# Leaving out the unread products in the two rests between an output product and its norm

## The chip, the cores and the metric

The kernel runs on one core of a Trainium2 chip. The metric is the device time of one execution in microseconds (us). TensorE (PE), VectorE (DVE), ScalarE (ACT) and GpSimd (POOL) each work through a stream of their own and meet at semaphores; SyncE (SP) issues the loads of the weights.

## The reference

The input is 256 tokens of width 2048, with 16 tokens set before them. Two blocks follow one another. What matters here is the end of the first block's mixer and the whole of its feed-forward part:

```
m = hybrid_mixer(rmsnorm(h, g_pre_mix), ...)      # ends in  y @ w_out
h = h + rmsnorm(m, g_post_mix)
f = conv_gated_ffn(rmsnorm(h, g_pre_ffn), ...)    # ends in  (...) @ w_down
h = h + rmsnorm(f, g_post_ffn)
x = h[:, 16:]
h2 = rmsnorm_2(x, norm_mix_g_2)                   # second block: attention branches, expert lookup
```

with `rmsnorm(x, g) = x * rsqrt(mean(x * x) + eps) * g` over the 2048 features of a token. Everything is float32.

## The kernel before

Features lie on partitions and tokens along the free axis, so a matrix product gives 128 output features by up to 272 tokens. The weights stream through four buffers of 128 x 1024 elements (some of 128 x 896). ACT rounds each of these chunks to a high part (`cut` of ACT, line 2430), DVE computes the low part (`cut` of DVE, line 1582), and PE forms each product in three passes: high by high, high by low, low by high (function `three`, lines 985 to 987). ACT may start chunk i only when PE has finished chunk i - 3 (semaphore `gemm`), PE needs both parts (`lo`). One engine's instructions run in the order in which they are written out; there is no scheduler.

A norm that stands behind a whole output needs all 16 row tiles before the next product can start. There are two such places, which the text calls rest 1 (behind `w_out` of the first block, lines 1188 to 1194) and rest 2 (behind `w_down`, lines 1220 to 1226). In each:

1. ACT reads the last output tile, once squared and once scaled (lines 2596, 2597).
2. PE sums the squares over the features, token by token, with products one column wide (`token_squares`, line 1010).
3. ACT takes the root (`token_root`, line 2454), DVE the reciprocal (line 1623), and DVE writes it on a diagonal (line 1627).
4. PE multiplies ones by the diagonal, which puts each token's factor on all partitions in bank 7 (`spread_factor`, line 1018).
5. DVE scales a row and adds it to the residual (`post_row`, lines 1631, 1633), ACT and DVE split the normed row in high and low (lines 2442, 1590), and PE starts the next product with it (`by_rows`: for each of 16 rows, seven output tiles of three passes; it waits on `xlo`).

`keep_busy(o, n)` (line 989) issues n products of the 128 x 128 tile of ones with itself into a bank that nothing reads. It is called with 12 at the very start of the kernel, and in each rest once between steps 2 and 4 (3 products) and once behind step 4 (5 in rest 1, 8 in rest 2). A float32 product of this kind is two instructions in the profile, so 3, 5 and 8 products are 6, 10 and 16 instructions.

Of the kernel before, what the change touches and what calls it, by code (L numbers as in the profile page):

```python
# [506 lines left out]
def build(nc, A, out):  # L507
# [35 lines left out]
    ps = [top.enter_context(nc.psum_tensor(f"ps{i}", [128, 512], F32)) for i in range(8)]  # L543
# [439 lines left out]
    def _(t):  # L983
# [5 lines left out]
        def keep_busy(o, n):  # L989

            for _ in range(n):
                t.matmul(o, ones[:], ones[:], start=True, stop=True)  # L992
# [14 lines left out]
        def token_squares(T, row):  # L1007

            for b, (c, n) in enumerate(blocks(T)):
                last = t.matmul(ps[7][:, b:b + 1], tmp[:, row, c + n - 128:c + n], ones[:, 0:1], start=row == 0 and b == 0, stop=row == 5 and b == len(blocks(T)) - 1)  # L1010
            if row == 5:
                last.then_inc(ms_mm, 1)

        def spread_factor(T, n):

            for b, (c, w) in enumerate(blocks(T)):
                t.wait_ge(diagonal, n + b + 1)
                last = t.matmul(ps[7][:, c:c + w], ones[:], tmp[:, 4, c:c + w], start=True, stop=True)
            last.then_inc(factor, 1)
# [169 lines left out]
        token_squares(TQ, 0)  # L1189
        t.wait_ge(o_sq, 16)  # L1190
        token_squares(TQ, 5)
        keep_busy(ps[6][:, 0:128], 3)
        spread_factor(TQ, 0)
        keep_busy(ps[6][:, 0:128], 5)


        def og(n):
# [23 lines left out]
        token_squares(S, 0)  # L1221
        t.wait_ge(o_sq, 32)
        token_squares(S, 5)
        keep_busy(ps[6][:, 0:128], 3)
        spread_factor(S, 3)
        keep_busy(ps[6][:, 0:128], 8)


        x3 = halves(2, S)
# [343 lines left out]
    def _(v):  # L1573
# [380 lines left out]
        def cos_2(x):  # L1954

            c, _, dst = rotation(x)
            if isinstance(x, tuple):
                v.wait_ge(up, 8 + x[1] + 1)
                v.tensor_tensor(dst, source2(x), c, ALU.mult).then_inc(own.up(), 1)
                return  # L1960
            if x == 0:
                v.wait_ge(made2, 3)
            name, h = TILES2[x]
            if name == "iq" and h >= 4:
                v.wait_ge(idx_s, h - 3)
            v.wait_ge(src, COPIED.index(x) + 1)
            o = ps[BANK2["in2", x]][:, 0:S]
            if name == "sk":
                v.scalar_tensor_tensor(dst, o, 128 ** -0.5, c, ALU.mult, ALU.mult).then_inc(ev2, 1)
            else:  # L1970
                v.tensor_tensor(dst, o, c, ALU.mult).then_inc(ev2, 1)

        def sin_2(x):

            _, s_, dst = rotation(x)
            r = ROPED.index(x)
            turned = swapped[r % NTURN]
            v.wait_ge(d_turn[r % NTURN], 16 * brought(x))
            v.tensor_tensor(turned, turned, s_, ALU.mult).then_inc(own.up(), 1)
            v.wait_ge(own.sem, own.n)  # L1980
            if not isinstance(x, tuple):
                v.wait_ge(ev2, READ2.index(("in2", x)) + 1)
            v.tensor_tensor(dst, dst, turned, ALU.add).then_inc(roped, 1)
# [436 lines left out]
    def _(s):  # L2420
# [252 lines left out]
        def side_2(name, a):  # L2673
# [24 lines left out]
            elif name == "relu":  # L2698
                s.wait_ge(idx_s, a + 1)
                if a >= 2:  # L2700
                    s.wait_ge(idx_w, 4 * (a - 1))
                for i in range(2):
                    s.activation(relu_at(2 * a + i, 0, 384), ps[7 - i][:, 0:384], ACT.Relu).then_inc(idx_r, 1)
            elif name == "exp":
                bs, _, pw, _, st = unit2(a)
                if a >= 2:
                    s.wait_ge(turn2, a - 1)
                s.wait_ge(rowmax2, 2 * a + 2)
                for n, (o, nk) in enumerate(VIEW2):
                    s.activation(pw[:, o:o + nk], bs[:, o:o + nk], ACT.Exp, bias=st[:, 2 * n:2 * n + 1],  # L2710
                                 accum_out=st[:, 2 * n + 1:2 * n + 2]).then_inc(expd2, 1)
            elif name == "scale":
                _, _, pw, _, st = unit2(a)
                s.wait_ge(inv2, 2 * a + 2)
                for n, (o, nk) in enumerate(VIEW2):
                    last = s.activation(pw[:, o:o + nk], pw[:, o:o + nk], ACT.Copy, scale=st[:, 2 * n + 1:2 * n + 2])
                last.then_inc(normed2, 1)
            elif name == "tcopy":
                _, bt, _, pT, _ = unit2(a)
                s.wait_ge(turn2, a + 1)  # L2720
                if a >= 2:
                    s.wait_ge(mixed2, a - 1)
                s.copy(pT, bt[:, 0:384]).then_inc(pt2_ok, 1)
            elif name == "high":
                s.wait_ge(mixed2, a + 1)
                s.copy((oa if a < 8 else ob)[0][:, a % 8, :], mixed_at(a)).then_inc(o_h, 1)
# [374 lines left out]
```

## Time and profile before

| what | us |
|---|---|
| median of 3 runs | 3157.22 |
| lowest, highest | 3156.95, 3158.32 |
| the profiled execution | 3157.26 |
| its span, first to last instruction | 3155.5 |
| PE busy in the span | 3144.1 |
| DVE busy | 2146.6 |
| ACT busy | 1822.5 |

The busy time of PE is that of overlapping instructions: a product of 256 columns is recorded as 0.28 us long, while the next one starts about 0.12 us after it. So the pace of PE is read from the starts, and a full busy share doesn't mean that nothing is lost. The granted clock in the views is the share of full speed at which TensorE's clock was granted: 1.00 is 2.4 GHz and 0.50 is 1.2 GHz.

### The profile page before, as it was taken

The page shows a single profiled execution, that of the slowest core. Times are in us where ns is not written, and L with a number is a line of the kernel's source. Part 1 is how long each engine was busy: PE and PEld are TensorE (multiplying, and loading weights), DVE is VectorE, ACT ScalarE, POOL GpSimd, SP SyncE. Part 2 cuts the span into 40 slices and gives each one's busy share as a digit, 9 for nine tenths or more (in the row PEclk, how much of TensorE's full clock was granted, in tenths as well). Part 3 has the DMA queues.
Part 4 walks back from the last instruction along what each step waited for, and adds up shares of the span by engine and source line. Part 5 has one row for each costly group of instructions (what it writes and reads, how often), then busy time and mean ns, then how long its engine had stood idle before and what let it go on. Part 6 is the DMA issues. An engine that isn't in the chain of part 4 may idle for free.

```text
span 3155.5 us, 58852 instructions
## 1 busy us (share of the span) xinstructions
PE 3144.1 (100%) x24162; PEld 3005.8 (95%) x24162; DVE 2146.6 (68%) x3502; ACT 1822.5 (58%) x2610; POOL 455.7 (14%) x313
## 2 busy tenths in 40 slices
PE   9999999999999999999999999999999999999999
PEld 9999999999999999999999999999999888888887
DVE  7987486666665477665666799855555666668887
ACT  6556464444444455555455578877777544446555
POOL 0001200000000000000000056777771000000000
PEclk9999999999999999999999999999999999999999
DMA  6444557666666656544565577788776777766655
GB/s 227 155 148 134 184 182 231 229 224 229 226 201 195 193 172 207 171 157 167 186 197 198 200 190 195 197 194 194 195 194 194 243 242 241 242 227 224 211 187 173
DMA packets 229564, 627.78 MB, mean 199 GB/s; under 512 B 59344, under 2 KB 78896, under 8 KB 229168
## 3 DMA queue, kind: packets, MB, share of 16 engines
q1 hardware_dynamic: 192000, 623.15, 60.4%
q0 software_dynamic: 36864, 0.15, 3.4%
q8 instruction: 192, 3.15, 0.4%
q10 hardware_dynamic: 432, 0.72, 0.1%
q14 instruction: 76, 0.62, 0.1%
HBM read 601.27 MB, written 21.10 MB: 197 GB/s over the span
## 4 chain that ended last, share of the span: by engine, by line
PE 98%; DVE 1%; ACT 0%; issue 0%; POOL 0%; DVEq 0%; ACTq 0%; POOLq 0%
PE ps L985 32%; PE ps L986 32%; PE ps L987 32%; PE ps L1061 0%; PE ps L992 0%; DVE wl L1582 0%; PE ps L1327 0%; PE ps L1267 0%; PE ps L1065 0%; PE ps L1026 0%; PE ps L1313 0%; PE ps L1286 0%; PE ps L1295 0%; PE ps L1069 0%; PE ps L1119 0%
## 5 line engine op out<-in xcount | busy, mean ns | idle before, releaser
L2430 ACT CAST wh<-raw 128x1024 fp32r<-128x1024 f32 (+3 forms) x1094 | 1137.4, 1040 | 1026.1 <-PE ps L987 1006.7
L1582 DVE TENSOR_TENSOR wl<-raw,wh 128x1024 fp32r<-128x1024 f32 (+2 forms) x863 | 1036.9, 1202 | 366.5 <-ACT wh L2430 364.0
L985 PE MATMUL ps<-xh,wh 128*128 128x256 f32 x3088 | 853.9, 277 | 0.5 <-issue 0.5
L987 PE MATMUL ps<-xh,wl 128*128 128x256 f32 x3088 | 850.1, 275 | 0.0
L986 PE MATMUL ps<-xl,wh 128*128 128x256 f32 x3088 | 850.0, 275 | 0.0
L985 PE MATMUL ps<-xw,wh 128*128 128x258 f32 (+2 forms) x2096 | 591.3, 282 | 1.1 <-issue 1.1
L987 PE MATMUL ps<-xw,wl 128*128 128x258 f32 (+2 forms) x2096 | 588.0, 281 | 0.0
L985 PEld LDWEIGHTS ps<-xh,wh 128*128 128x128 f32 x3088 | 579.7, 188 | 1.9 <-issue 0.7
L986 PEld LDWEIGHTS ps<-xl,wh 128*128 128x128 f32 x3088 | 579.8, 188 | 0.1
L987 PEld LDWEIGHTS ps<-xh,wl 128*128 128x128 f32 x3088 | 579.6, 188 | 0.0
L2960 POOL DMA_INDIRECT table<-w_loose x256 | 397.7, 1553 | 806.6 <-DVE w_loose L2257 651.3
L1582 DVE TENSOR_TENSOR wl<-raw,ph 128x1024 fp32r<-128x1024 f32 x231 | 281.3, 1220 | 224.3 <-ACT ph L2435 199.6
L986 PE MATMUL ps<-xw,wh 128*128 128x258 f32 (+2 forms) x1441 | 404.5, 281 | 0.0
L985 PEld LDWEIGHTS ps<-xw,wh 128*128 128x128 f32 x2096 | 394.5, 188 | 1.6 <-issue 1.2
L987 PEld LDWEIGHTS ps<-xw,wl 128*128 128x128 f32 x2096 | 394.3, 188 | 0.0
L986 PE MATMUL ps<-wl,coefs 128*128 128x512 f32 x941 | 365.9, 389 | 0.0
L987 PE MATMUL ps<-wh,coefs 128*128 128x512 f32 x941 | 365.9, 389 | 0.0
L985 PE MATMUL ps<-wh,coefs 128*128 128x512 f32 x941 | 365.9, 389 | 0.0
L986 PEld LDWEIGHTS ps<-xw,wh 128*128 128x128 f32 x1441 | 270.8, 188 | 0.1
L2435 ACT CAST ph<-raw 128x1024 fp32r<-128x1024 f32 x231 | 232.6, 1007 | 0.0
L985 PEld LDWEIGHTS ps<-wh,coefs 128*128 128x128 f32 x941 | 176.6, 188 | 36.7
L987 PEld LDWEIGHTS ps<-wh,coefs 128*128 128x128 f32 x941 | 176.6, 188 | 36.6
(409 smaller groups left out, 4647.3 us busy)
## 6 DMA issues: line engine op xcount, KB each, us to landing
raw<-in_peer_u SPq DMA_DIRECT2D x256, 512.0 KB
raw<-in_peer_v SPq DMA_DIRECT2D x236, 512.0 KB
raw<-in_w_in SPq DMA_DIRECT2D x172, 512.0 KB
raw<-in_w_up SPq DMA_DIRECT2D x82, 512.0 KB
raw<-in_w_gate SPq DMA_DIRECT2D x80, 512.0 KB
raw<-in_w_down SPq DMA_DIRECT2D x80, 512.0 KB
raw<-in_w_out SPq DMA_DIRECT2D x64, 512.0 KB
table<-tmp SPq DMA_DIRECT2D x32, 512.0 KB, 6.6
```

The lines of the kernel that those rows point to most:

```text
L985: t.matmul(o, lh, rh, start=start, stop=False)
L986: t.matmul(o, lh, rl, start=False, stop=False)
L987: return t.matmul(o, ll, rh, start=False, stop=stop)
L1582: v.tensor_tensor(part_at(wl, i), raw[:, i % RN, 0:cols(i)], high.bitcast(F32), ALU.subtract).then_inc(lo, 1)
L2430: last = s.copy(part_at(wh, i), raw[:, i % RN, 0:cols(i)])
L2435: last = s.copy(ph[:, 2 + i % 2, :], raw[:, i % RN, 0:cols(i)])
L2960: g.indirect_dma_start(out=table, out_offset=bass.IndirectOffsetOnAxis(ap=eidx[q][:, n:n + 1], axis=0), in_=wts[q][:, n:n + 1], in_offset= ...
```

## The change

The four calls of `keep_busy` in the two rests are left out. The one at the start of the kernel stays. No wait, no buffer and no other instruction is touched.

```diff
         token_squares(TQ, 0)
         t.wait_ge(o_sq, 16)
         token_squares(TQ, 5)
-        keep_busy(ps[6][:, 0:128], 3)
         spread_factor(TQ, 0)
-        keep_busy(ps[6][:, 0:128], 5)
...
         token_squares(S, 0)
         t.wait_ge(o_sq, 32)
         token_squares(S, 5)
-        keep_busy(ps[6][:, 0:128], 3)
         spread_factor(S, 3)
-        keep_busy(ps[6][:, 0:128], 8)
```

## Rows read from the trace of the kernel before

**Rows 1.** The page: busy time of PE, and the last chain by engine.
```profile
PE 3144.1 (100%) x24162; PEld 3005.8 (95%) x24162; DVE 2146.6 (68%) x3502; ACT 1822.5 (58%) x2610; POOL 455.7 (14%) x313
...
PE 98%; DVE 1%; ACT 0%; issue 0%; POOL 0%; DVEq 0%; ACTq 0%; POOLq 0%
```

**Rows 2.** Waits of PE, whole span: in total, times, longest.
```profile
PE ps L985 <- issue: 1.6, 2, 1.1
...
PE ps L1018 <- DVE tmp L1627: 0.4, 2, 0.2
```

**Rows 3.** Timeline of rest 1: start, length, engine, line, tiles, [idle before].
```profile
397.74 1.47 PE L1010 MATMUL ps<-ones,tmp 128*128 128x1 f32 x12
...
399.07 0.91 PE L992 MATMUL ps<-ones 128*128 128x128 f32 x6
...
399.87 0.62 DVE L1627 TENSOR_SCALAR tmp<-ident,col 128x128 f32<-128x128 f32 x3
...
400.21 0.83 PE L1018 MATMUL ps<-tmp,ones 128*128 128x128 f32 x6 [0.22 <-DVE tmp L1627]
...
400.90 1.36 PE L992 MATMUL ps<-ones 128*128 128x128 f32 x10
401.14 0.42 DVE L1631 TENSOR_TENSOR mt<-mt,ps 128x258 f32<-128x258 f32 x1 [0.66 <-PE ps L1018]
...
402.75 0.48 DVE L1590 SCALAR_TENSOR_TENSOR xw<-ht,par,xw 128x258 fp32r<-128x258 f32 x1
...
403.33 0.36 PE L985 MATMUL ps<-xw,wh 128*128 128x258 f32 x1 [1.07 <-issue]
```

**Rows 4.** Timeline of rest 2.
```profile
1135.59 0.91 PE L992 MATMUL ps<-ones 128*128 128x128 f32 x6
...
1136.37 0.48 DVE L1627 TENSOR_SCALAR tmp<-ident,col 128x128 f32<-128x128 f32 x2
...
1136.71 0.71 PE L1018 MATMUL ps<-tmp,ones 128*128 128x128 f32 x4 [0.21 <-DVE tmp L1627]
...
1137.26 1.95 PE L992 MATMUL ps<-ones 128*128 128x128 f32 x16
...
1139.12 0.48 DVE L1590 SCALAR_TENSOR_TENSOR xl<-ht,par,xh 128x256 fp32r<-128x256 f32 x1
...
1139.70 0.36 PE L985 MATMUL ps<-xh,wh 128*128 128x256 f32 x1 [0.49 <-issue]
```

**Rows 5.** Stretches: length, busy PE, PEld, DVE, ACT, POOL, granted clock, DMA.
```profile
402.30:403.30 1.00, 0.00 (x0) 0.00 (x1) 0.97 (x4) 0.71 (x2) 0.00 (x0) 1.00 0.00 0
...
1139.20:1139.70 0.50, 0.01 (x1) 0.03 (x1) 0.50 (x3) 0.46 (x1) 0.00 (x0) 1.00 0.98 401
```

**Rows 6.** Stretches behind the last product of the kernel.
```profile
3148.10:3150.40 2.30, 0.01 (x1) 0.00 (x0) 1.80 (x7) 1.83 (x7) 0.00 (x0) 1.00 0.87 314
...
3150.50:3150.60 0.10, 0.00 (x0) 0.00 (x0) 0.10 (x1) 0.10 (x2) 0.00 (x0) 0.79 0.95 369
...
3150.70:3155.50 4.80, 0.00 (x0) 0.00 (x0) 0.79 (x2) 0.58 (x1) 0.00 (x0) 0.50 0.64 231
```

**Rows 7.** Timeline of PE at the start of the kernel.
```profile
1.02 5.49 PE L992 MATMUL ps<-ones 128*128 128x128 f32 x24 [1.02 <-POOL ones L2915]
...
6.58 0.43 PE L986 MATMUL ps<-xw,wh 128*128 128x272 f32 x1
6.80 0.33 PE L987 MATMUL ps<-xw,wl 128*128 128x272 f32 x1
...
7.09 0.29 PE L986 MATMUL ps<-xw,wh 128*128 128x272 f32 x1
7.21 0.29 PE L987 MATMUL ps<-xw,wl 128*128 128x272 f32 x1
```

**Rows 8.** Waits of DVE, then of PE, from 1139.7 to 1177 us.
```profile
DVE wl L1582 <- ACT wh L2430: 0.5, 1, 0.5
...
PE ps L1026 <- DVE mt L1604: 0.4, 1, 0.4
```

## The prediction

> **What bounds the kernel now.** I read four views. First the page: PE is busy for 3144.1 us of 3155.5 and makes up 98% of the chain that ended last [rows 1]. So whatever PE loses is lost to the kernel, and whatever another engine does faster is hidden unless PE waits for it. Second, PE's waits over the whole span: apart from the start of the kernel there is almost nothing. The two waits of line 985, 1.6 us together, and the two of line 1018, 0.4 us together, are the ones that matter here [rows 2], and they are the two rests. Third, the timeline of each rest, to see who releases whom. Fourth, the stretches with the granted clock, because products that nobody reads can have only two effects: they hold up what is queued behind them on PE, or they keep PE active.
>
> What the reader is to see in rest 1 [rows 3]: the squares run from 397.74; the six unread instructions begin at 399.07 and last 0.91, so they end at 399.98. DVE begins the diagonal at 399.87, and the spreading products start at 400.21. They wait 0.22 us for DVE. DVE's first scaled row starts at 401.14, when the spread is done (400.21 + 0.83 = 401.04). The low part of the first normed row is finished at 402.75 + 0.48 = 403.23, and the first product starts at 403.33. The ten unread instructions are over at 400.90 + 1.36 = 402.26, so PE has stood still for 1.07 us when it resumes. Rest 2 is the same [rows 4]: the unread instructions end at 1135.59 + 0.91 = 1136.50, the spread starts at 1136.71, the second batch ends at 1137.26 + 1.95 = 1139.21, the low part is finished at 1139.12 + 0.48 = 1139.60 and the first product starts at 1139.70.
>
> **Part one: what the removed instructions held up.** There are 6 + 10 + 6 + 16 = 38 of them, with recorded stretches of 0.91 + 1.36 + 0.91 + 1.95 = 5.13 us of PE time. None is on the path. The batch before the spread ended 0.23 us (rest 1) and 0.21 us (rest 2) before the spread started, and the spread was released by DVE [rows 3, 4]. The batch behind it ended 1.07 and 0.49 us before the products, which were waiting for DVE's low part. That part started from the spread's end, which doesn't move. Bank 6, which they wrote, is read by nobody here, and DVE reads the factors in bank 7. So the gain is 0.00 us. From below I allow 0.1 us of gain for each rest, the hand-over that lies between the end of DVE's low part and PE's start (403.23 to 403.33, 1139.60 to 1139.70), as a bound for any small effect on PE's queue. I take 0: the wait ends with DVE whether PE was busy before it or not.
>
> **Part two: what PE does instead.** Without them PE is still from the end of the squares to the first product, except for the spread. In rest 1 that is 399.07 to 403.33 = 4.26 us, of which the spread takes 0.83, and the last unbroken gap is 403.33 - 401.04 = 2.29 us. In rest 2 it is 1135.59 to 1139.70 = 4.11 us with 0.71 of spread, and the last gap is 1139.70 - 1137.42 = 2.28 us. Before, the unread instructions left gaps of 1.07 and 0.49 us, and the clock was at 1.00 even in those gaps, which is the level of 2.4 GHz [rows 5].
>
> The trace has one place where PE stops behind full-rate work and stays still: the end of the kernel. From 3148.10 on there is no product. The granted clock is 1.00 until 3150.40, 0.79 in the tenth from 3150.50 to 3150.60, and 0.50, the level of 1.2 GHz, from there on [rows 6]. A share of 0.79 in that tenth puts the step at 3150.56. So the clock fell 2.46 us after the last product. The gaps of 2.29 and 2.28 us are a little shorter, but each stands behind only six or four spreading instructions and another gap of about 1 us, where the end of the kernel had dense products before it. Taken over the whole rest PE is idle for 4.26 - 0.83 = 3.43 and 4.11 - 0.71 = 3.40 us, more than the 2.46 that were enough. I take it that the clock falls in both rests, with a chance of 7 in 10.
>
> The Trainium skill, "TensorE: Matmul & The Clock Gate", section "Why this matters for your kernels", advises against gaps between bursts of matmuls only when they are longer than the last gaps here; read literally it would leave the clock at its high level and the sum at 3157.3. The rows at the kernel's end disagree with that reading, since there 2.46 us were enough.
>
> **Price of a fall.** At the start of the kernel PE runs from 1.02 us at half pace: 24 unread instructions before the first real one at 6.18 are 5.16 / 24 = 0.215 us apart, and the products of 272 columns at 6.58 and 6.80 are 0.22 apart. Those at 7.09 and 7.21 are 0.12 apart [rows 7]. (The granted-clock record has no step there; the spacing shows it.) So PE worked for about 5.9 us, 1.02 to 6.9, before it had its full pace. At half pace a stretch of length c does the work of c / 2, so c / 2 is lost. From above a fall costs 5.9 / 2 = 2.95 us. From below it costs 0, when the clock is back as the products resume. The start is the nearest row and the only one, but it is a single reading of something whose timing against the products I can't see, so I don't take it as a constant. I take the middle between the whole and the half of it, c = 4.4 us, or 2.2 us for each rest. If the clock falls before the spread, the spread takes up to twice its time on top: 0.83 and 0.71 us more at most. I take 0 for it and keep it for the upper end.
>
> **What hides a part.** In rest 2's ramp PE later waits 0.4 us for DVE's sums (line 1604) [rows 8]; a PE that comes later would wait less, if DVE doesn't come later too. But DVE is held by PE there: it waited 0.5 us for ACT's high part, which itself waits for PE to finish a row. With PE at half pace DVE stalls at the same place, and the rows behind it in its order stall too. So between 0 and 0.4 us are given back; I take 0.2, halfway, and nothing for rest 1.
>
> **Sum.** 0 + 2.2 + 2.2 - 0.2 = +4.2 us. The profiled execution took 3157.26 us, 1.76 outside its span of 3155.5, and stands 0.04 over the median of the runs, so 3157.26 + 4.2 = 3161.46, and against the median 3161.4. I predict 3161.4 us, 0.13% over the kernel before.
>
> **The rivals.** A measurement of this kernel can tell about 0.2% from no change, which is 6.3 us.
>
> Rival A, not slower: the clock stays at its high level in both rests. For it: the longest unbroken gaps, 2.29 and 2.28 us, are under the 2.46 us of the end, and the spread between the gaps is work. Against it: the idle time of a rest adds up to 3.4 us. Time 3157.2 us, 3157.0 to 3157.3 with the 0.2 us of possible gain. It decides if the spread and the gap lengths are enough activity. Chance 0.12.
>
> Rival B: only one of the rests loses the clock, or it falls in one execution and not in the other, because the two gaps are nearly as long as the bound. Time 3157.2 + 2.2 = 3159.4, 3158.5 to 3160.2. Chance 0.13.
>
> Rival C, clearly slower: the fall comes early, before the spread, in both rests, and each then costs the start's whole 2.95 us plus the slowed spread: 2 x 2.95 + 0.83 + 0.71 = 7.4, or 3164.7 us. For it: between the squares, which are one column wide, and the spread PE is idle for over 1 us more than it is now. Against it: the clock at the end held for 2.46 us, and from the last dense product at 397.74 to the spread at 400.21 it is 2.47 us, so it would be just at the edge, twice. It crosses 0.2% from 3163.5 on. Chance 0.10.
>
> Rival D, faster: the unread instructions held the spread or the products up in a way that the timeline hides, such as the queue of weight loads. It is worth at most 5.13 us, all of their time, if both were wrongly read, or 3152.1 us. The starts follow DVE's ends by 0.1 us in both rests, which leaves no room for it. Chance 0.01.
>
> **How the numbers follow.** The likeliest case, both rests losing the clock, has 0.64: the same steps with c from 2.9 us (2 x 1.45 - 0.2 = 2.7) to 5.9 us (2 x 2.95 = 5.9) give 3159.9 to 3163.1. Cases A, B and the forecast together have 0.89, and a range from 3156.9 to 3163.8 holds them and the nearer half of C; what is left out is well under 2 in 10, but the low end can't be raised without losing A and the upper bound is set by the price of two falls. Over 0.2% slower: C, 0.10, and a tail of 0.02 of the forecast, so 0.12. Over 0.2% faster: D, and 0.01 for what I don't see, so 0.02. Within 0.2%: 0.86.
>
> **What would show it.** In the profile of the changed kernel: the spread starts released by DVE's diagonal, at the same distance from the squares as before (part one). PE has a gap of about 2.3 us before the first product of each ramp. The granted clock shows 0.50 there or just after it, for 3 to 6 us, and the products in that stretch start about 0.22 us apart instead of 0.12. From the ramps' ends on everything is as before, shifted by 4 us. If the clock is 1.00 throughout both rests and the span is 3155.5, the forecast is wrong and rival A holds. If the spread itself is twice as long, rival C has begun. If the first product of a ramp comes earlier after the squares than before, part one is wrong. If the gap at line 1026 in rest 2's ramp is gone, the part given back is larger than my 0.2.

## The result: 4.2 us slower, and the profile after

| | before | after |
|---|---|---|
| median of 20 runs, us | 3157.21 | 3161.44 |
| lowest, highest | 3156.47, 3158.49 | 3160.22, 3162.45 |
| the profiled execution | 3157.26 | 3161.32 |
| its span | 3155.5 | 3159.5 |
| granted clock, mean | 0.999 | 0.998 |

The ratio is 1.0013, with a 95% interval of 1.0008 to 1.0019: 0.13% slower, within the 0.2% that the prediction called no change, but clear of 1. No execution of after is as fast as the slowest of before. The mean granted clock is 0.997 or 0.998 in each of the twenty executions of after, and 0.999 or 1.000 in each of the 102 executions of the kernel before that were run beside the experiments. The forecast was 3161.4.

PE's busy time and its waits over the whole span of after, against [rows 1, 2]:

```profile
PE 3143.2 (99%) x24124; PEld 3005.2 (95%) x24124; DVE 2146.5 (68%) x3502; ACT 1822.3 (58%) x2610; POOL 456.5 (14%) x313
```
```profile
PE ps L985 <- issue: 4.6, 2, 2.3
PE ps L1018 <- DVE tmp L1623: 2.0, 2, 1.0
```

There are 38 PE instructions fewer, 24124 for 24162. The waits that they covered now show: 4.6 us ahead of the ramps for 1.6, and 2.0 us ahead of the spreads for 0.4. (The ramp is the run of products that starts behind a rest.) These waits cost nothing, since the same time was there before with unread work in it. The loss is in what follows. The timeline of rest 1 in after, against [rows 3] (lines stand up to four lower than before: 1586 is the low part of a normed row, 1590 before, and 1623 the diagonal, 1627 before):

```profile
397.40 1.47 PE L1010 MATMUL ps<-ones,tmp 128*128 128x1 f32 x12
...
399.87 0.83 PE L1018 MATMUL ps<-tmp,ones 128*128 128x128 f32 x6 [1.00 <-DVE tmp L1623]
...
402.40 0.48 DVE L1586 SCALAR_TENSOR_TENSOR xw<-ht,par,xw 128x258 fp32r<-128x258 f32 x1
...
402.99 0.55 PE L985 MATMUL ps<-xw,wh 128*128 128x258 f32 x1 [2.29 <-issue]
403.33 0.42 PE L986 MATMUL ps<-xw,wh 128*128 128x258 f32 x1
403.55 0.42 PE L987 MATMUL ps<-xw,wl 128*128 128x258 f32 x1
...
407.62 0.33 PE L985 MATMUL ps<-xw,wh 128*128 128x258 f32 x1
407.79 0.28 PE L986 MATMUL ps<-xw,wh 128*128 128x258 f32 x1
407.91 0.28 PE L987 MATMUL ps<-xw,wl 128*128 128x258 f32 x1
```

From the squares to the first product it is 402.99 - 397.40 = 5.59 us, as before (403.33 - 397.74 = 5.59). Then the products start 0.22 us apart where they were 0.12 apart. The stretches of both rests show why (length, busy PE, PEld, DVE, ACT, POOL, granted clock, DMA):

```profile
400.00:400.80 0.80, 0.70 (x6) 0.61 (x6) 0.15 (x2) 0.00 (x0) 0.00 (x0) 1.00 0.00 0
400.80:401.00 0.20, 0.00 (x0) 0.00 (x0) 0.19 (x1) 0.00 (x0) 0.00 (x0) 0.72 0.00 0
401.00:407.00 6.00, 4.01 (x19) 4.05 (x20) 5.14 (x12) 1.53 (x3) 0.00 (x0) 0.50 0.15 37
...
407.60:407.80 0.20, 0.20 (x4) 0.20 (x3) 0.00 (x0) 0.00 (x0) 0.00 (x0) 0.71 0.32 126
407.80:410.00 2.20, 2.20 (x21) 2.20 (x20) 1.11 (x2) 2.08 (x3) 0.00 (x0) 1.00 0.02 7
...
1141.50:1141.70 0.20, 0.20 (x2) 0.20 (x3) 0.17 (x2) 0.00 (x0) 0.00 (x0) 0.70 0.00 0
1141.70:1144.90 3.20, 3.20 (x17) 3.20 (x16) 2.94 (x6) 0.51 (x1) 0.00 (x0) 0.50 0.21 23
1144.90:1145.10 0.20, 0.20 (x3) 0.20 (x3) 0.00 (x0) 0.00 (x0) 0.00 (x0) 0.77 0.35 90
```

The granted clock fell to 0.50, which is 1.2 GHz, in both rests. A stretch that shows 0.72 was at the low level for 2 x 0.28 of its length, so the fall in rest 1 was at 400.89 and the return at 407.72; in rest 2 the fall was at 1141.58, just behind the first product at 1141.40, and the return at 1144.99. Products worked at the low level for 4.7 us in the first case (from 402.99) and 3.4 us in the second.

Where the 4.0 us of span come from is told by the distances between five marks on PE, which are differences of starts in the timelines:

| | before | after |
|---|---|---|
| start to first square of rest 1 | 397.74 | 397.40 |
| rest 1, to the first product | 5.59 | 5.59 |
| from there to the squares of rest 2 | 731.15 | 733.20 |
| rest 2, to the first product | 5.22 | 5.21 |
| from there to the last product | 2008.13 | 2010.42 |

The two rests are unchanged. Each stretch behind a rest is longer, by 2.05 and 2.29 us, and most of that lies in its first microseconds: the 22nd product of ramp 1 starts 4.63 us behind the first for 2.55 (407.62 - 402.99 against 405.88 - 403.33), and the 18th of ramp 2 starts 3.60 behind it for 2.04, so 2.08 and 1.56 us. The last stretch differs by another 0.7 us. Nearly all of it lies in one place, 112 us behind rest 2, where the same 140 products take 16.49 us for 15.87 at a granted clock of 1.00 (the first of them and the one that follows the last, before and then after):

```profile
1252.10 0.28 PE L986 MATMUL ps<-oal,wh 128*128 128x256 f32 x1
...
1267.97 0.28 PE L985 MATMUL ps<-oah,wh 128*128 128x256 f32 x1
```
```profile
1255.36 0.28 PE L986 MATMUL ps<-oal,wh 128*128 128x256 f32 x1
...
1271.85 0.28 PE L985 MATMUL ps<-oah,wh 128*128 128x256 f32 x1
```

That is 0.118 us between starts for 0.113. Each of the thirteen traces of this study has one of these two lengths there: 15.87 in before, e5, e9 and e10, 16.49 in the other nine. All seven traces with a fall have the longer one, but so have e7 and e11, whose rests are at full clock. So it doesn't need a fall; whether a fall makes it likelier isn't shown. Over the eight traces with rest 2 at full clock the last stretch lies between 2008.10 and 2009.08 us.

### The profile page after: what moved, and what is told of

Read it like the earlier page. It is cut to its first block, busy times and chain, and to the rows that moved or that the text cites. A ratio compares the mean times of both kernels' runs of the same rounds, so it can differ in the third digit from the quotient of the medians.

```text
span 3159.5 us, 58776 instructions
## 1 busy us (share of the span) xinstructions
PE 3143.2 (99%) x24124; PEld 3005.2 (95%) x24124; DVE 2146.5 (68%) x3502; ACT 1822.3 (58%) x2610; POOL 456.5 (14%) x313
## 4 chain that ended last, share of the span: by engine, by line
PE 98%; DVE 1%; ACT 0%; issue 0%; POOL 0%; DMA 0%; DVEq 0%; SPq 0%; ACTq 0%; POOLq 0%
PE ps L985 32%; PE ps L986 32%; PE ps L987 32%; PE ps L1061 0%; DVE wl L1578 0%; PE ps L1323 0%; PE ps L1263 0%; PE ps L1065 0%; PE ps L1026 0%; PE ps L1309 0%; PE ps L1282 0%; PE ps L1291 0%; PE ps L1069 0%; PE ps L1119 0%; PE ps L1470 0%
## 5 line engine op out<-in xcount | busy, mean ns | idle before, releaser
L2426 ACT CAST wh<-raw 128x1024 fp32r<-128x1024 f32 (+3 forms) x1094 | 1137.1, 1040 | 1030.0 <-PE ps L987 1027.6
L986 PEld LDWEIGHTS ps<-wl,coefs 128*128 128x128 f32 x941 | 176.7, 188 | 36.6
L985 PEld LDWEIGHTS ps<-wh,coefs 128*128 128x128 f32 x941 | 176.7, 188 | 36.6
```

The lines of the kernel that those rows point to most:

```text
L985: t.matmul(o, lh, rh, start=start, stop=False)
L986: t.matmul(o, lh, rl, start=False, stop=False)
L2426: last = s.copy(part_at(wh, i), raw[:, i % RN, 0:cols(i)])
```

## Experiments

What is open is when the clock falls. Two theories: T, the last unbroken gap ahead of the products decides; U, the idle time of the whole rest decides. All runs have 11 timed executions; before has 33 beside the first four and the next four, 21 beside e9 and e10 and 15 beside e11.

### e1 and e2: one batch of unread products kept, the other gone

```diff
 e1, rest 1 (rest 2 alike)            e2, rest 1 (rest 2 alike)
         keep_busy(..., 3)           -        keep_busy(..., 3)
         spread_factor(TQ, 0)                 spread_factor(TQ, 0)
-        keep_busy(..., 5)                    keep_busy(..., 5)
```

> The three unread products ahead of the spread stay in both rests, the ones behind it go. Theory T (the last unbroken gap decides): the gap of 2.3 us ahead of the first product of each ramp is as in the changed kernel, so the clock falls in both rests and the time is that of the changed kernel, 3160.9 to 3161.7 us. Theory U (the idle time of the whole rest decides): idle time per rest is 4.3 - 0.8 - 0.9 = 2.6 us, nearly the 2.46 us after which the clock fell at the kernel's end, so it falls in some executions only: 3158 to 3160 us. If the clock is 1.00 through both rests, 3157.2 us, both are wrong on this.

> The five and eight unread products behind the spread stay, the three ahead of it go. Theory T (the last unbroken gap decides): that gap is 1.07 and 0.49 us as before the change, the clock holds and the time is 3157.2 us. Theory U (idle time of the whole rest): 1.1 + 1.07 = 2.2 us in rest 1 and 1.1 + 0.49 = 1.6 us in rest 2, under 2.46, so it holds as well, 3157.2 us. Over 3158.5 us would speak against both, and say that the front batch is what holds the clock.

Measured: e1 3161.14 us (3160.04 to 3162.04), ratio 1.0012 [1.0003, 1.0021]; e2 3158.96 us (3156.80 to 3160.81), ratio 1.0004 [0.9995, 1.0013]; before 3157.43. So e1 is nearly the changed kernel again, +3.7 us for +4.2: three products ahead of the spread save little or nothing. That is what T expected. But e2 fails both theories. It has the short last gaps of the kernel before, and its executions lie over 4 us. In its profiled one, of 3158.96 us, the clock fell in both rests, and in rest 1 it fell while the unread products were running (timeline, then stretches):

```profile
400.57 2.09 PE L992 MATMUL ps<-ones 128*128 128x128 f32 x10
402.99 0.55 PE L985 MATMUL ps<-xw,wh 128*128 128x258 f32 x1 [0.34 <-issue]
...
1136.97 0.71 PE L1018 MATMUL ps<-tmp,ones 128*128 128x128 f32 x4 [0.99 <-DVE tmp L1625]
1137.52 2.92 PE L992 MATMUL ps<-ones 128*128 128x128 f32 x16
1140.09 0.56 PE L985 MATMUL ps<-xh,wh 128*128 128x256 f32 x1
```
```profile
400.50:400.90 0.40, 0.40 (x6) 0.40 (x6) 0.09 (x1) 0.00 (x0) 0.00 (x0) 1.00 0.00 0
400.90:401.10 0.20, 0.20 (x4) 0.20 (x3) 0.20 (x1) 0.00 (x0) 0.00 (x0) 0.75 0.00 0
...
1138.40:1141.60 3.20, 3.20 (x17) 3.20 (x17) 3.13 (x8) 1.52 (x3) 0.00 (x0) 0.50 0.33 126
```

The reader is to see that the ten instructions take 2.09 us where they took 1.36 [rows 3], and that the sixteen of rest 2 now outlast the gap: the ramp starts 1140.09 - 1134.74 = 5.35 us behind the squares for 5.22. So the fall answers to what came earlier, and the last gap (0.34 us, and none in rest 2) doesn't decide it. T doesn't hold. U's number is wrong as well, since the idle time of e2 was under 2.46 us. What remains of U is that both batches count.

The falls aren't in every execution of e2. Of its eleven, the three fastest, 3156.80 to 3157.56 us, have a mean granted clock of 1.000, the next two 0.999, and the six from 3158.96 us up 0.998. So the time goes with the clock within one kernel too.

### e3 and e4: one rest bare, the other as before

```diff
 e3: rest 1 without both calls, rest 2 as before
 e4: rest 1 as before, rest 2 without both calls
```

> The unread products go in rest 1 only. If the loss is local to each rest (the clock's price), this run costs rest 1's share, 2.4 us by the cold products of the changed kernel (402.99 to 407.72 at half pace), so 3159.6 us, and rest 2 is as in the kernel before. Rival: the loss comes from something that the two rests share or that runs on (the order of loads, a lag of DVE that is made good only later), and then this run has all of it, 3161.4 us, or none.

> The unread products go in rest 2 only. Local theory: 1.7 us, from the products that run at half pace in the changed kernel (1141.58 to 1145.0), up to 2.1 us as the median over executions, so 3158.9 to 3159.3 us, and this and the run with rest 1 bare add up to the changed kernel's 4.2 us. Rival: they don't add up (0 or 4.2 us here).

Measured: e3 3159.88 us (3158.35 to 3160.34), ratio 1.0007 [0.9998, 1.0016]; e4 3159.72 us (3158.21 to 3160.67), the same ratio and interval; before 3157.43. Each costs about half, +2.45 and +2.29, together 4.7 against the 4.2 of both at once, as near as medians that move by half a microsecond allow. The loss is local to each rest, and in the trace of each the clock leaves 1.00 only there, apart from the kernel's end. In e3's trace the low level lasted from 402.30 to 409.12, so products worked at it for 5.96 us, and the stretch from the first product to the squares of rest 2 is 733.76 us long for 731.15. e4's profiled execution lost it early (stretches and timeline):

```profile
1136.40:1136.60 0.20, 0.13 (x1) 0.14 (x1) 0.20 (x2) 0.20 (x1) 0.00 (x0) 0.66 0.00 0
1136.60:1143.20 6.60, 4.32 (x19) 4.06 (x20) 5.28 (x13) 1.53 (x4) 0.00 (x0) 0.50 0.31 86
```
```profile
1136.47 1.22 PE L1018 MATMUL ps<-tmp,ones 128*128 128x128 f32 x4 [0.99 <-DVE tmp L1625]
...
1139.96 0.55 PE L985 MATMUL ps<-xh,wh 128*128 128x256 f32 x1 [2.28 <-issue]
```

Here the spread takes 1.22 us for 0.71 and the rest is 1139.96 - 1134.24 = 5.72 us long for 5.22, all of it on the path. That is the slowed spread of rival C. e6's trace has a slight case of it: the fall came at 400.46, in the spread of rest 1, which took 0.91 us for 0.83.

### e5: far more unread products than fit

```diff
-        keep_busy(ps[6][:, 0:128], 5)      # rest 1, behind the spread
+        keep_busy(ps[6][:, 0:128], 19)
-        keep_busy(ps[6][:, 0:128], 8)      # rest 2, behind the spread
+        keep_busy(ps[6][:, 0:128], 20)
```

> The kernel before with 19 and 20 unread products behind the spread in place of 5 and 8: 28 and 24 instructions more, at 0.12 and 0.112 us 3.4 and 2.7 us of PE time. PE stood still 1.07 and 0.49 us there, so if unread products cost only what outlasts that gap, the ramps start 2.3 and 2.2 us late: 3157.4 + 4.5 = 3161.9 us at an undisturbed clock. Rival: PE had more room than the gaps show (it waits for DVE later in the ramps, so a late start is made good): 3157.4 to 3159 us. Rival: unread products cost their whole time anyway, 6.1 us, 3163.5 us.

Measured: 3161.25 us (3161.00 to 3162.97), ratio 1.0012 [1.0003, 1.0021]; before 3157.58, so +3.7. The clock stays at 1.00 up to the kernel's end. The ramps start at once behind the unread instructions (rest 1, then rest 2):

```profile
400.93 4.49 PE L992 MATMUL ps<-ones 128*128 128x128 f32 x38
405.17 0.37 PE L985 MATMUL ps<-xw,wh 128*128 128x258 f32 x1
...
1139.01 4.63 PE L992 MATMUL ps<-ones 128*128 128x128 f32 x40
1143.39 0.36 PE L985 MATMUL ps<-xh,wh 128*128 128x256 f32 x1
```

The rests are 7.40 and 7.16 us long for 5.59 and 5.22, +1.81 and +1.94, and nothing is made good later (731.06 and 2008.10 us for the stretches behind them). My 4.5 was too high, mostly since the end of a recorded product isn't the time at which the next may start: a product recorded as 0.275 us long is followed after 0.112, so PE has 0.16 us more room in each rest than its record shows. Another 0.2 us is that I took 0.12 us for an instruction in rest 1, where it is 0.112. The last 0.1 us of each rest stays open. So unread products are free while they fit and cost their time beyond that, which is what part one of the prediction rests on.

### e6: half of the unread products

```diff
-        keep_busy(..., 3)  spread_factor(TQ, 0)  keep_busy(..., 5)
+        keep_busy(..., 1)  spread_factor(TQ, 0)  keep_busy(..., 2)
-        keep_busy(..., 3)  spread_factor(S, 3)   keep_busy(..., 8)
+        keep_busy(..., 1)  spread_factor(S, 3)   keep_busy(..., 4)
```

> The kernel before with 1 and 2 products in rest 1 and 1 and 4 in rest 2, in place of 3 and 5, 3 and 8. If the clock's fall is a matter of degree, of how much of a rest PE works, this falls in most executions but not all, and costs between the run with only the products behind the spread (3159.0) and the changed kernel (3161.4): 3159.5 to 3161 us. Rival: few products suffice, if they only break the gaps up: 3157.4 to 3158 us.

Measured: 3159.57 us (3159.34 to 3162.15), ratio 1.0008 [0.9999, 1.0017]; before 3157.58. Eight of eleven executions lie between 3159.34 and 3159.91 and three from 3161.28 up. In the profiled one the clock fell in rest 1 and held in rest 2:

```profile
402.00:407.00 5.00, 3.96 (x18) 4.00 (x19) 4.22 (x10) 1.31 (x3) 0.00 (x0) 0.50 0.16 25
...
1136.00:1139.00 3.00, 2.21 (x18) 1.93 (x17) 1.62 (x4) 1.84 (x4) 0.00 (x0) 1.00 0.33 128
1139.00:1142.00 3.00, 1.62 (x14) 1.46 (x13) 2.84 (x8) 1.06 (x3) 0.00 (x0) 1.00 0.56 166
```

So half the filling gives back about half of the loss, and in the trace it does so because one rest lost the clock and the other kept it. No execution is as fast as the slowest of the kernel before, 3158.97 us, and the three slow ones have a mean granted clock of 0.997 for 0.998 or 0.999. That fits a fall in rest 1 each time and in rest 2 sometimes, but only the profiled execution shows where the falls are.

### e7, e8 and e11: the high parts first

Of the 21 passes of a ramp's first row only seven need DVE's low part of that row. Seven others need the high parts alone, and seven the low part of the weights. The edit puts them in that order, so that PE can start before DVE has finished:

```diff
+                early = norm > 0 and k == 0
+                if early:
+                    t.wait_ge(xhi, 16 * norm + 1)
+                    t.wait_ge(hi, i0 + 1)
+                    for n in range(ROWS):      # high by high
+                        t.matmul(outs[n], row_at(wh, i0, n), rhs[n % 2](0)[0], start=True, stop=False)
+                    taken(i0)
+                    for n in range(ROWS):      # low part of the weights
+                        t.matmul(outs[n], row_at(wl, i0, n), rhs[n % 2](0)[0], start=False, stop=False)
                 t.wait_ge(xlo, 16 * norm + k + 1)
+                if early:                      # low part of the row
+                    for n in range(ROWS):
+                        last = t.matmul(outs[n], row_at(wh, i0, n), rhs[n % 2](0)[1], start=False, stop=False)
...
```

e7 and e11 are this in the kernel before, e8 is this in the changed kernel.

> The kernel before with all its unread products, and in the two ramps the first row's 21 passes in another order: the seven high by high ones first, which need only ACT's high part of the row, then the seven with the weights' low part, then the seven that need DVE's low part. ACT's high part is done at 402.07 + 0.51 = 402.58 and 1138.45 + 0.51 = 1138.96, DVE's low part at 403.23 and 1139.60. So PE can start 0.65 us earlier in rest 1 and, as the unread products end at 1139.21, 0.4 us earlier in rest 2. If nothing behind holds PE, the kernel is 1.0 us faster, 3156.4 us. Rival: PE gets ahead but then waits for DVE's second row or low part of the weights, and nothing is gained: 3157.4 us.

> The same new order of the first row's passes in the changed kernel, without unread products in the rests. The last gap shrinks from 2.3 to 1.6 us in both rests. If the clock's fall hangs on that last gap, it now holds often and the time is under 3158.5 us. If it hangs on the activity of the rest as a whole, the clock falls as before and the time is the changed kernel's less the 1.0 to 1.3 us of the earlier start: 3160.2 us.

> The kernel of the run with the high parts first once more, in a new set of runs. If its gain of 1.2 us was real and is that of the two earlier starts (0.85 and 0.4 us or less), it is again 0.7 to 1.3 us under the kernel before. If it was the luck of one set of executions, 0 to 0.4 us.

Measured: e7 3156.37 us (3155.36 to 3157.12), before 3157.58, ratio 0.9995 [0.9986, 1.0004]; e11 3155.96 us (3155.52 to 3156.77), before 3157.16, ratio 0.9996 [0.9987, 1.0005]; e8 3160.31 us (3158.95 to 3161.18), before 3157.58, ratio 1.0008 [0.9999, 1.0017]. e7's timeline (line 1040 is the first seven passes):

```profile
397.54 1.47 PE L1010 MATMUL ps<-ones,tmp 128*128 128x1 f32 x12
...
400.69 1.36 PE L992 MATMUL ps<-ones 128*128 128x128 f32 x10
402.47 1.07 PE L1040 MATMUL ps<-xw,wh 128*128 128x258 f32 x7 [0.42 <-issue]
...
1133.61 1.24 PE L1010 MATMUL ps<-ones,tmp 128*128 128x1 f32 x8
...
1138.18 1.06 PE L1040 MATMUL ps<-xh,wh 128*128 128x256 f32 x7
```

The rests are 4.93 and 4.57 us long, 0.66 and 0.65 shorter than in the kernel before, 1.31 together. Both sets gave 1.2 us under their runs of before, and in e11 only one of eleven executions isn't under the lowest of before. This is the fastest version of the study by its medians, but each interval includes 1, so a change of 0.04% isn't settled by either interval alone. e8 lies 1.1 us under the changed kernel. Not all of that need be the earlier start, since the low level lasted 3.4 us in both rests of e8's trace, where it was 6.8 and 3.4 us in that of after. Last gaps of 1.64 us for 2.29 didn't hold the clock.

### e9 and e10: the gaps filled to the brim

```diff
 e9 (e7's order):    3 -> 4 ahead of the spreads, 5 -> 7 and 8 behind
 e10 (before's):     3 -> 4 ahead of the spreads, 5 -> 9 and 8 -> 10 behind
```

> The order of the first row's passes of the run with the high parts first, and the rests filled as far as they go without touching the path: four unread products ahead of the spread in place of three, seven behind it in rest 1 in place of five, eight in rest 2 as before. If some executions of the kernel before still lose the clock for a moment in a rest (its times spread over 2 us, those of the overfilled run over half a us but for one), filling holds it, and the median comes down to the low end of the run with the high parts first, 3155.5 to 3155.9 us, with a narrower spread. Rival: the spread comes from elsewhere (the start), and the time is that run's, 3156.4 us. Rival: the fourth product touches the spread and costs up to 0.2 us in each rest.

> The kernel before with four unread products ahead of the spread and nine and ten behind it, in place of three, five and eight, which fills the gaps without outlasting them by more than 0.1 us. If a fuller rest is safer, 3156.8 to 3157.0 us with a narrow spread; if the rests of the kernel before already hold the clock always, 3157.4 us as before.

Measured: e9 3156.76 us (3155.82 to 3157.53), ratio 0.9999 [0.9990, 1.0008]; e10 3157.93 us (3156.66 to 3158.43), ratio 1.0002 [0.9993, 1.0011]; before 3157.01. Neither is better than the kernel that it fills, and neither spread is narrower, so the guess that the kernel before still loses the clock at times has nothing for it. In e9's trace the rests are 4.94 and 4.57 us long, as in e7, so the fourth product didn't touch the spread. Yet its median is only 0.25 us under its runs of before, where e7 and e11 have 1.2; no run here shows where the other 0.95 us are. In e10's trace the rests are as in before (5.59 and 5.22 us); it starts rest 1 0.23 us later, and its last stretch is 2009.05 us, 0.9 more. Nearly all of that lies between 1209 and 1219 us, where PE waits once for DVE's low part of the weights, which it didn't in before (PE's waits from 1200 to 1240 us):

```profile
PE ps L985 <- DVE wl L1582: 0.4, 1, 0.4
```

Whether the other executions of e10 have it too isn't shown.

## Why the prediction was right, step by step

- **Part one, nothing gained.** Right. The rests kept their lengths to 0.01 us, and e5 shows the reverse, that unread products cost only what outlasts the gap. Rival D is out.
- **Part two, the clock falls in both rests.** Right in the result: the granted clock says so in both, and the slowest time of before lies under the fastest of after. Its reason was only partly right. I leaned on the gaps as against the 2.46 us at the kernel's end [rows 6], and e2 and e8 show that a gap's length is not the measure: the clock fell with last gaps of 0.34 and 1.64 us, in e2 even under running products. The total idle time was the better guide, but not with 2.46 us as its bound. That was one reading of something that varies. Behind the last product, which is the same in all thirteen traces, the clock fell between 2.08 us (e5) and 5.07 us (e10) later. In e10 the last product ends at 3148.95 + 0.28 = 3149.23, and the step is at 3154.30:

```profile
3149.30:3154.20 4.90, 0.00 (x0) 0.00 (x0) 2.86 (x7) 2.64 (x8) 0.00 (x0) 1.00 0.84 303
3154.20:3154.40 0.20, 0.00 (x0) 0.00 (x0) 0.00 (x0) 0.00 (x0) 0.00 (x0) 0.76 1.05 374
```

  The rests say the same. In rest 1 without unread products the fall came 3.49 us behind the start of the squares in after and 4.73 in e3, and in rest 2 5.39 us in after and 2.22 in e4. So the moment of a fall isn't set by the rest alone, and what else sets it stays open. The prediction had no such term: by its reason e2 was expected to keep the clock. What the runs show is an order. With all the unread products no trace has a fall in the rest. With half of them, or those behind the spread alone, the clock falls in some cases. With those ahead alone, or none, every such rest has one, and the medians are 3.7 and 4.2 us over their runs of before. "TensorE: Matmul & The Clock Gate" of the Trainium skill warns, under "Why this matters for your kernels", of long idle gaps between bursts. The trace of after already goes beyond that, since no gap in it is longer than 2.29 us, and by e2 a rest of short gaps with some work between them lost the clock too.
- **The price, 2.2 us each.** Right in size as a mean, since e3 and e4 cost 2.45 and 2.29 us by their medians, but too high for this trace. I took 4.4 us at the low level; the trace of after has 4.7 and 3.4 us of products at it, and the other traces have from 1.4 us (e2, rest 1) to 6.0 us (e3). The low level itself lasted 6.8 us in rest 1, longer than the 3 to 6 us that the prediction named as the sign. The 4.4 us came from two bounds at the kernel's start, so that it fell near the middle of these is luck. And I took half of it as lost. Measured is 2.08 and 1.56 us, or 0.44 and 0.46 of it, because the products' starts went from about 0.12 to 0.214 us apart, which is less than double. Both errors make the forecast too high in rest 2, and the two nearly cancel in rest 1. The Trainium skill's page of the same title gives, in "Wait — 56ns, not 53.3ns?", N / 1.2 GHz between starts at the low level and N / 2.4 GHz with 2.5 ns more at the high one, which makes an estimate of 215 and 110 ns for 258 columns. The trace agrees with the first; the products here are 120 ns apart at the high one, and that is why a fall costs less than half.
- **0.2 us given back in rest 2's ramp.** Wrong, it was nothing. PE's wait for DVE's sums is there as before, 0.4 us, and DVE has waited for ACT's high part for 2.0 us in its place. These are the waits of after from 1141 to 1181 us, PE's and then DVE's, for [rows 8]:

```profile
PE ps L1026 <- DVE mt L1600: 0.4, 1, 0.4
```
```profile
DVE wl L1578 <- ACT wh L2426: 2.0, 1, 2.0
```

  DVE was held back as much as PE was, by the chain that the prediction named as the reason against giving back. The whole of the lag came through.
- **The slowed spread, 0 in the sum.** Right for the profiled execution, where the fall came behind the spread. e4 has it at 0.5 us and e6 at 0.1, so it happens in some executions and belongs to the spread of the times. Rival C's premise was also misread: PE waits 1.00 us ahead of the spread for 0.22, which is 0.8 us more and not over 1 us.
- **The sum.** The trace's own sum is 2.08 + 1.56 = 3.64 us, less 0.34 at the start, plus 0.7 in the last stretch, of which 0.6 is the slower stretch at 1252 us: 4.0. The medians say 4.2. The prediction had neither of the last two terms, so that it met the medians to 0.1 us is luck in part.

## What to carry to other kernels

Work that nobody reads kept TensorE at its high clock here through rests that other engines set the length of. It cost nothing while it fitted, and its absence cost 2 us for each rest. Judge such filler by the whole rest, not by its last gap, and test it by taking away each batch alone, because a batch behind the middle of the rest didn't do without the one ahead of it. Don't take the moment of a fall from one trace: look at several executions and their granted clocks. Once a rest is full enough to hold the clock, shorten it instead of filling it further: starting the first products on the operand that is ready first took 0.65 us off each rest in the traces.

## What the runs showed of the hardware that was not expected

- The clock can fall while products run. In e2 it fell at 401.0, in the middle of ten instructions that took 2.09 us for 1.36.
- At the low level products of 258 columns started 0.214 us apart, at the high one 0.12: a factor of 1.8, not 2.
- The low level lasted 6.8 us in rest 1 of after (400.89 to 407.72) and 3.4 us in rest 2 (1141.58 to 1144.99), and the other traces with a fall show one or the other of these two lengths: 6.8 in e1's, e3's and e6's rest 1 and e4's rest 2, 3.4 in both rests of e2 and e8 and in e1's rest 2.
- Behind the same last product the clock fell after 2.08 us in one trace and after 5.07 us in another.
- At a granted clock of 1.00 the same 140 products took 15.87 us in four traces and 16.49 in nine, with nothing between.
- The start of the kernel varies from one execution to the next: the first square of rest 1 stood between 397.37 and 397.97 us in the thirteen traces.
